# A two-block transformer on one core: in-projection norms applied after the matmuls, and new addresses for the split halves

## What is computed

```python
for layer in range(2):
    h = rms_norm(x, g_mix[layer])        # x * rsqrt(mean(x*x) + 1e-6) * g
    qkv = h @ w_in[layer]                # 1024 -> 3072
    ...                                  # three kinds of attention
    x = x + mix @ w_out[layer]
    h2 = rms_norm(x, g_ffn[layer])
    x = x + conv_gated_mlp(h2, ...)      # up 1024 -> 5632, down 2816 -> 1024
x = rms_norm(x, g_final)
```

## Time and profile before

| | us |
|---|---|
| median of 3 executions | 1744.21 (1742.28 to 1744.73) |
| the profiled execution | 1744.4 |
| its span, first to last instruction | 1742.6 |
| TensorE (PE) busy | 1693.9 |
| VectorE (DVE) busy | 1151.4 |
| ScalarE (ACT) busy | 821.4 |
| GpSimd (POOL) busy | 706.1 |
| mean granted clock of TensorE, share of full | 0.996 |

### The profile page before, as it was taken

How to read it: one execution, slowest core, us unless ns; L and a number is a source line. 1 busy time by engine, 2 the same in 40 slices (tenths; PEclk the granted TensorE clock), 3 DMA queues, 4 the chain that set the end, 5 groups by cost and what they waited for, 6 DMA issues and landing times.

```text
span 1742.6 us, 27224 instructions
## 1 busy us (share of the span) xinstructions
PE 1693.9 (97%) x10714; PEld 1456.7 (84%) x10714; DVE 1151.4 (66%) x2422; ACT 821.4 (47%) x1453; POOL 706.1 (41%) x384
## 2 busy tenths in 40 slices
PE   7999999999999998999999999999999999999997
PEld 6779998777799986544579999999999988888885
DVE  6755785756467585655332999999999644444443
ACT  5555655355476642122343554544444455555553
POOL 2424676133266811421163999700000144444443
PEclk9999999999999999999999999999999999999998
DMA  7333545463165463323353656544444466666664
GB/s 289 117 109 135 191 170 183 148 217 117 61 211 201 170 199 122 107 86 120 97 202 114 225 165 203 179 144 141 144 145 140 162 193 194 194 193 194 194 193 134
DMA packets 77456, 283.20 MB, mean 163 GB/s; under 512 B 8721, under 2 KB 8977, under 8 KB 77073
## 3 DMA queue, kind: packets, MB, share of 16 engines
q1 hardware_dynamic: 76032, 276.50, 48.5%
q10 hardware_dynamic: 1296, 4.97, 0.8%
HBM read 279.33 MB, written 2.10 MB: 161 GB/s over the span
## 4 chain that ended last, share of the span: by engine, by line
PE 79%; DVE 7%; POOL 4%; ACT 4%; issue 3%; DMA 1%; POOLq 0%; DVEq 0%; ACTq 0%
PE bank L542 63%; PE bank L533 8%; PE bank L597 5%; POOL wl L2117 4%; ACT wh L1112 2%; DVE att L1478 2%; PE bank L665 1%; DVE wl L1461 1%; ACT att L1115 1%; PE bank L967 1%; PE bank L889 1%; DVE ssb L1467 1%; DVE mix L1506 1%; DVE xs L1467 1%; PE bank L837 0%
## 5 line engine op out<-in xcount | busy, mean ns | idle before, releaser
L2117 POOL TENSOR_TENSOR wl<-raw,wh 128x1024 fp32r<-128x1024 f32 x213 | 547.6, 2582 | 696.5 <-ACT wh L1112 688.1
L542 PE MATMUL bank<-hh,wh 128*128 128x256 f32 x1856 | 526.5, 284 | 5.1 <-POOL wl L2117 4.2
L1112 ACT ACTIVATE wh<-raw 128x1024 fp32r<-128x1024 f32 x476 | 492.9, 1050 | 58.2 <-PE bank L542 39.4
L542 PE MATMUL bank<-hl,wh 128*128 128x256 f32 x1856 | 519.3, 280 | 0.0
L542 PE MATMUL bank<-hh,wl 128*128 128x256 f32 x1856 | 517.9, 279 | 0.0
L1461 DVE TENSOR_TENSOR wl<-raw,wh 128x1024 fp32r<-128x1024 f32 x263 | 353.8, 1351 | 93.8 <-ACT wh L1112 93.3
L542 PEld LDWEIGHTS bank<-hh,wh 128*128 128x128 f32 x1856 | 349.1, 188 | 6.6 <-POOL wl L2117 5.5
L542 PEld LDWEIGHTS bank<-hl,wh 128*128 128x128 f32 x1856 | 349.2, 188 | 0.0
L542 PEld LDWEIGHTS bank<-hh,wl 128*128 128x128 f32 x1856 | 349.0, 188 | 0.0
L1467 DVE TENSOR_TENSOR acl<-H,ach 128x256 fp32r<-128x256 f32 x128 | 87.6, 685 | 181.5 <-ACT ach L1115 181.5
L542 PE MATMUL bank<-wh,ach 128*128 128x512 f32 x512 | 199.2, 389 | 0.4 <-DVE acl L1467 0.4
(11 more groups left out here) (216 smaller groups left out, 2322.5 us busy)
## 6 DMA issues: line engine op xcount, KB each, us to landing
raw<-in_ut_dram SPq DMA_DIRECT2D x128, 512.0 KB, 3.5
raw<-in_vt_dram SPq DMA_DIRECT2D x128, 512.0 KB, 3.7
raw<-in_wup_dram SPq DMA_DIRECT2D x88, 512.0 KB, 4.1
raw<-in_win_dram SPq DMA_DIRECT2D x48, 512.0 KB, 4.6
raw<-in_wdown_dram SPq DMA_DIRECT2D x44, 512.0 KB, 4.2
raw<-in_wout_dram SPq DMA_DIRECT2D x24, 512.0 KB, 3.6
raw<-in_wga_dram SPq DMA_DIRECT2D x16, 512.0 KB, 3.6
raw<-in_wpq_dram SPq DMA_DIRECT2D x16, 512.0 KB, 4.7
```

The lines of the kernel that those rows point to most:

```text
L542: m = p.e.matmul(out, lhs[i][a], rhs[i][b], start=start and i == 0 and j == 0, stop=stop and i == n - 1 and j == 2)
L1112: a.e.activation(high_of(u), raw_of(u), ACTF.Copy).then_inc(act_hi.up(("hi", u)), 1)
L2117: g.e.tensor_tensor(low_of(u), raw_of(u), high_of(u).bitcast(F32), ALU.subtract).then_inc(pool_lo.up(("lo", u)), 1)
```

## The change

Norm of x before the in projections: the row of weights is no longer multiplied in before the turning. x itself is turned; the weight enters as one column per 128 features (gcol, a new input of 128 x 32 floats) while the halves are made, ACT by a scale and DVE in one scalar_tensor_tensor; that makes one instruction per 128 x 128 block instead of one per 256 or 512 columns. The root per token enters when the in projection's result is evicted. The two rows leave the plan of units. In layer 0 slab 0 is no longer skewed, and 16 further transposes whose result nobody reads are issued behind the turning. Between the layers, tile 0 is turned inside the down projection, before the last unit's matmuls of tile 1 are complete.

Addresses: hh and hl become 9216 bytes each, of which the "f" halves (up projection, pq, ut) use the part from float 16 on and all others the part from 0. sta becomes 3072 bytes, con 6656, sml 3584; a tile gcol of 384 bytes stands ahead of xs; the reserve for dynamic DMA at the partition's start is 1024 bytes (it was 16384 by default).

```diff
-def program(nc, x_d, pos_d, consts_d, smalls_d, win_d, ...
+def program(nc, x_d, pos_d, consts_d, smalls_d, gcol_d, win_d, ...
+        gcol_s = scoped(ctx, "gcol", 96)
...
-        hh, hl = scoped(sc_h, "hh", 2048, F32R), scoped(sc_h, "hl", 2048, F32R)
+        hh, hl = scoped(sc_h, "hh", 2304, F32R), scoped(sc_h, "hl", 2304, F32R)
         sc_h.close()
-        hw, sel_s = scoped(ctx, "hw", 2048), scoped(ctx, "sel_s", 2048)
-        sta = scoped(ctx, "sta", 760)
+        hw, sel_s = scoped(ctx, "hw", 2304), scoped(ctx, "sel_s", 2304)
+        sta = scoped(ctx, "sta", 768)
...
-        con_s = scoped(early, "con", K_W - 128)
-        sml_s = scoped(early, "sml", S_W)
+        con_s = scoped(early, "con", 1664)
+        sml_s = scoped(early, "sml", 896)
...
         for L in range(DEPTH):
-            stage(("row", "n", L), [(rows_d[L], 1024, False)])
...
-                lower.append("pd"[i % 2])
+                lower.append("dp"[i % 2])
...
+        def hT_of(st):
+            o = 16 if st[0] == "f" else 0
+            return [w[:, o:o + 2048].rearrange("p (k t) -> p k t", k=8) for w in (hh, hl)]
+
+        def gcol(st, k):
+            return gcol_s[:, 8 * (st[1] + 2 * (st[0] == "f")) + k:8 * (st[1] + 2 * (st[0] == "f")) + k + 1]
...
+            def x_turned(st, t, k0, b, *after):
+                claim(b)
+                p.wait_ge(*after)
+                n = block_of(st, t, k0)[1]
+                for k in range(k0, k0 + n):
+                    m = p.e.transpose(banks[b][:, (k - k0) * 128:(k - k0) * 128 + 128], x[:, t, k * 128:(k + 1) * 128], ids[:, :])
+                m.then_inc(pe_out.up(("T", st, t, k0)), 1)
...
             p.wait_ge(id_in, "id")
-            turned(("n", 0), mix, 8, (0, 1), lambda t, q: (dve_out, ("nrm", ("n", 0), t, q)))
+            for q in range(2):
+                for t in range(2):
+                    x_turned(("n", 0), t, 4 * q, 2 * q + t, (x0_in, x1_in)[t], "x")
+            turn[0] += 6
+            kept_streaming(16, 5)
...
-                                  lambda n, t: (act_out if t else dve_out, ("ev", "win", L, n, t)), of=slab_banks, skew=(0,),
-                                  between=(lambda: turned(("n", 1), mix, 8, (1,), ...)) if L else None, at=(3, 0))
+                                  lambda n, t: (act_out if t else dve_out, ("ev", "win", L, n, t)), of=slab_banks, skew=(0,) if L else (),
+                                  between=(lambda: [x_turned(("n", 1), 1, 4 * q, rot(), dve_out, ("xd", 0, 1, q)) for q in range(2)]) if L else None, at=(3, 0))
...
+                        if L == 0 and (f, t, n) == (NTILE - 2, 1, 0):
+                            spare = [(acc[1][1] + i) % 8 for i in (1, 2)]
+                            for q in range(2):
+                                x_turned(("n", 1), 0, 4 * q, spare[q], dve_out, ("xd", 0, 0, q))
...
+            def x_high(st, t, ks):
+                for k in ks:
+                    a.wait_ge(pe_out, ("T", st, t, block_of(st, t, k)[0]))
+                    a.wait_ge(g_in, "g")
+                    do(hT_of(st)[0][:, k, tcols(t)], turned_block(st, t, k), ACTF.Identity, ("hTh", st, t, k), scale=gcol(st, k))
...
             load(ids[:, :], consts_d[:, 0:128], id_in, "id")
+            load(gcol_s[:, 0:32], gcol_d, g_in, "g")
             load(pos_i, pos_d, pos_in, "pos")
             for t in range(2):
+                x_high(("n", 0), t, range(4))
+            stream_up_to(first["win", 0] + 1)
+            load(con_s[:, 0:K_W - 128], consts_d[:, 128:K_W], con_in, "con")
+            load(sml(0, S_W), smalls_d, sml_in, "sml")
+            for t in range(2):
+                x_high(("n", 0), t, range(4, 8))
+            stream_up_to(first["win", 0] + 2)
+            for t in range(2):
                 squares(("n", 0), t, x[:, t, :], mix[:, t, :], 0, (x0_in, x1_in)[t], "x")
-            stream_up_to(first["win", 0])
-            load(con_s[:, :], consts_d[:, 128:K_W], con_in, "con")
-            load(sml(0, S_W), smalls_d, sml_in, "sml")
-            turned(("n", 0), (0, ), 2)
-            stream_up_to(first["win", 0] + 1)
-            turned(("n", 0), (1, ), 2)
-            stream(0)
...
                         a.wait_ge(pe_out, ("mm", ("win", L), k // 4, 1))
-                        do(qkv[:, 1, ...], ps(("win", L), k // 4, 1), ACTF.Copy, ("ev", "win", L, k // 4, 1))
+                        a.wait_ge(pool_out, ("rs", ("n", L), 1))
+                        do(qkv[:, 1, ...], ps(("win", L), k // 4, 1), ACTF.Identity, ("ev", "win", L, k // 4, 1), scale=rstd[:, 1:2])
...
+            def x_low(st, t, ks):
+                for k in ks:
+                    v.wait_ge(act_out, ("hTh", st, t, sum(block_of(st, t, k)) - 1))
+                    v.wait_ge(g_in, "g")
+                    v.e.scalar_tensor_tensor(hT_of(st)[1][:, k, tcols(t)], turned_block(st, t, k), gcol(st, k), hT_of(st)[0][:, k, tcols(t)].bitcast(F32),
+                                             ALU.mult, ALU.subtract).then_inc(dve_out.up(("hT", st, t, k)), 1)
...
             for t in range(2):
+                x_low(("n", 0), t, range(4))
+            stream_up_to(first["win", 0])
+            for t in range(2):
+                x_low(("n", 0), t, range(4, 8))
+            stream_up_to(first["win", 0] + 2)
+            for t in range(2):
                 mean(("n", 0), t, False)
-                scale(("n", 0), t, mix, first["row", "n", 0])
-            stream_up_to(first["win", 0])
-            turned(("n", 0), (0, 1), 2)
-            stream(0)
...
-                        copy(qkv[:, 0, ...], ps(("win", L), k // 4, 0), ("ev", "win", L, k // 4, 0), alone=True)
+                        v.wait_ge(pool_out, ("rs", ("n", L), 0))
+                        v.e.tensor_scalar(qkv[:, 0, ...], ps(("win", L), k // 4, 0), rstd[:, 0:1], None, ALU.mult
+                                          ).then_inc(dve_out.up(("ev", "win", L, k // 4, 0)), 1)
...
-            for t in range(2):
-                root(("n", 0), t)
-            g.wait_ge(dve_out, ("nrm", ("n", 0), 1, 1))
-            stream(0)
...
                     if k < 23:
                         stream(first["win", L] + k)
+                    if k == 0:
+                        if L == 0:
+                            root(("n", 0), 0)
+                        root(("n", L), 1)
...
-                            root(("n", 1), t)
-                            g.wait_ge(dve_out, ("nrm", ("n", 1), t, 1))
+                            if t == 0:
+                                root(("n", 1), 0)
...
-    nc = _bacc.Bacc("TRN2", target_bir_lowering=False, num_devices=1)
+    nc = _bacc.Bacc("TRN2", target_bir_lowering=False, num_devices=1, dynamic_dma_scratch_size=1024)
```

More of the change, by code:

```diff
@@ L250, in program @@
             else:
-                L = 0 if i < first["row", "n", 1] else 1
-                if first["row", "n", L] + 7 <= i < first["wdown", L] - 5 and not (L == 0 and i < first["win", 0] + 6):
+                L = 0 if i < first["win", 1] else 1
+                if first["win", L] + 6 <= i < first["wdown", L] - 5 and not (L == 0 and i < first["win", 0] + 6):
                     lower.append("ddp"[i % 3])
@@ L821, in pe @@
                 if L == 0:
-                    turned(("n", 1), mix, 8, (0,), lambda t, q: (dve_out, ("nrm", ("n", 1), t, q)), of=[b for b in range(8) if b not in acc[1]])
+                    turn[0] += 3
             turned_whole(("n", 2), hn2, (0, ))
```

93 lines of the change are left out of this document (51 added, 42 removed).

## The result

The changed kernel takes 1751.57 us (median of 6 executions, 1749.78 to 1757.73), the kernel before 1744.47 on the same chip (1741.94 to 1746.20): a ratio of 1.0056, 95% interval 1.0045 to 1.0067. The change makes it slower by 0.56% (0.41% by the medians; two of the six executions took over 1757 us), where I had forecast 1720 us. The profiled execution took 1749.78 us around its span of 1748.0; before it was 1744.4 around 1742.6.

A forecast was written before the change was run, and what follows sets the result against it. TensorE, busy 1693.9 of 1742.6 us, was taken to bound the kernel. The homes, entry and layer boundary terms sum to 24.2 us off the median of 1744.2, giving 1720 us, with a range of 1707 to 1745.

The forecast's parts named there:

- Homes: Address part: tiles starting at one place modulo 512 save some 7 ns per 512-column matmul; "f" halves sit 64 bytes off.
- (a): Down projections: the 512-column step falls from 233.4 and 228.3 to 226.6 ns, a gain of 2.7 us.
- (b): In and out projections: step from 233.4 to 226.6 ns; two thirds of 5.9 us taken, a gain of 3.9 us.
- Rival D: Everywhere: position has nothing to do with the step; 0.2 us left, 1744 us; chance 0.13.
- (c): "f" halves, 64 bytes off: 256-column step falls to 113.3 ns; gains: up projections 10.1 us, pq 1.8, ut 5.5.
- My discount for DVE: ut's other 69 units: half of their 7.4 us counted, because DVE is busy 40.0 of 40 us from 1260.
- Rival B: "f" halves: 64 bytes is like any other difference, 256-column steps stay at 118 ns; 1737 us; chance 0.20.
- Rival C: "f" halves: 64 bytes brings the full hindrance, 120.2 ns a step, so slower; 1750 us; chance 0.12.
- Entry: Kernel start through slab 0, with raw x turned and a wait for gcol: -0.7 us, between -2 and +1.7.
- Layer boundary: Between layers: no POOL wait for the scaled row, tile 0 turned in the down projection; TensorE's idle goes, 0.9 us gained.

The follow-up runs named there:

- homes_only: The kernel before with the new addresses alone ("f" halves at 64 bytes), old norms, plan and slots: 1738.41 us, ratio 0.9978.
- homes_192: The kernel before with the new addresses alone, but the "f" halves at 192 bytes instead of 64: 1737.38 us, ratio 0.9959.
- entry_repaired: slots_back with DVE's low half ahead of the small steps, ACT's sines one unit later, POOL only units 1 and 3 of the first 12: 1743.30 us.
- slots_back: The changed kernel with the unit slots ahead of ut moved back by two, as before the change: 1747.03 us, ratio 1.0016.
- halves_back: slots_back with each unit's low half made by the same engine as in the kernel before: 1744.81 us, ratio 1.0011.

## Why the prediction was wrong

- **Homes, (a) and (b).** Right in size of the step: 226.5 ns was measured for 226.6. The size: down projections 2.0 us (0.8 and 1.2 in homes_only) for 2.7, since layer 0 still waits 0.37 and 1.39 us for POOL. In and out projections some 1.7 us for 3.9 (0.35, 0.23, 0.11, 0.77 and 0.24 in the table's rows): attention paces more of them than the third I had taken. Rival D, that position does nothing, is out: by addresses alone (homes_only) the in projection's step went from 233.4 to 226.7 ns, 24 steps from 350.12 to 355.56 us. The Trainium skill (TensorE: Matmul & The Clock Gate, Step-by-step: what each phase is for) says that streamed data and weights come through two independent ports and loading weights takes nothing from the running matmul, which would have made D right; the measurement decides against it. How the two reads hinder each other no run shows.
- **Homes, (c), the step that failed.** I took 113.3 ns for the "f" halves at 64 bytes: I carried the floor from one form to the other and called every other difference a hindrance of one size. I also read one step per difference from the trace before, where ut already ran mostly at 116.7 ns, at the same 32 bytes as the up projection's 117.8 (96 steps):
```profile
1059.83 0.28 PE L542 MATMUL bank<-hh,wh 128*128 128x256 f32 x1
...
1071.03 0.28 PE L542 MATMUL bank<-hh,wh 128*128 128x256 f32 x1
```

There are at least five levels (113.3, 116.7, 117.8, 118.7, 120.0), and at 64 bytes two of them. Up projections: 0.4 us for 10.1. pq: 1.7 in homes_only for 1.8. ut: 3.3 won in its first part at 113.3, 1.55 lost in the rest, where the step went from 116.7 to 117.8, for 5.5. My discount for DVE there stays untested at the floor, but in homes_192, with every second unit at 113.3, TensorE had no wait from 1130 to 1370 us. Rival B was right about the up projections alone. Rival C had the right sign, and its 1750 us are within 2 us of the result by luck: 120.0 exists, but not at 64.
- **A gain that had no place to go.** In homes_192, where up projection 1 ran at 113.3, two thirds of it came back as waits for POOL one stage later; in entry_repaired, with other engines for the low halves, nothing did. I had asked what is late next for ut, and not for the up projection.
- **Entry.** First matmul 14.72 us for 14.2. gcol came at 8.9, not 9.8, but an ACT table load of 1.28 us stood behind it, which I had left out. Slab 0 ended at 25.8 for 26.8, better than forecast. The failed step is that I stopped the sum there: the loss of 4.35 us lies in slab 1, where unit 4's low half stood on DVE behind small steps slowed by POOL's two low halves, a queue I had not walked through. The half clock behind the wait was not in the sum.
- **Layer boundary.** Forecast +0.9. The first slab of layer 1 lost 2.66 us, because the halving of the rows stands in ACT's queue ahead of four wh's; the cover I had named (down matmuls and the slab) needs those wh's itself. Down projection 0 won more than the addresses give it, so that the two stages together gained 0.6 us over homes_only (76.63 to 76.04 in slots_back). But that gain is the shifted engines': with the engines as before (halves_back) the two take 78.37 us, a loss of 1.7.
- **Not in the sum at all.** Two units fewer in the plan shift every rule in `i % n`: the slots (7.2 us at ut's start, 4.5 of the median, 0.40% by the ratios) and the halves' engines (3.9 us at the entry and 4.0 at the attention's start, against 2.4 won in down projection 0; 2.2 of the median, 0.05% by the ratios). I put this at nothing without a reason. It takes the ratio from 1.0056 to 1.0011; what is left between that and homes_only's 0.9978 is the new norms' own entry (about 1 us up to slab 3), the boundary, levels of the step that differ by execution (1.7 us in pq), and a rest that the runs don't split.

## What to carry to other kernels

Taking an element out of a list whose consumers are chosen by `i % n` changes all that follow: print slots and engines of both versions and compare them before costing anything. A matmul's step depends on where its operands lie, and has to be measured for each form: the best difference of one form was among the worst of the other. A faster stage is worth only what its own supply and that of the next stage allow, so add up both before counting the gain.

## What was unexpected of the hardware

- Same form, same addresses modulo 512, granted clock 1.00, one execution: 113.3 ns in one stretch and 117.8 in another, each constant over hundreds of steps. At 64 bytes the level changed at waits or single long steps of TensorE, in both directions, and 22 extra matmuls did not change it; at 192 bytes it alternated from unit to unit, with eight short matmuls between and no wait.
- 256-column form: 120.0 ns at differences of 0, 96 and 256 bytes, 113.3 or 117.8 at 64 and 192; 512-column form: 226.6 at 0.
- Two DVE steps of 24 elements took 2.5 us while POOL made a low half, and 0.39 behind it. What looks like a bundle of cheap steps cost as much time as POOL's two low halves.
- The half clock lasted 3.4 us behind waits of 1.84 and 2.77 us, and 6.8 us at the wait of 6.99 us, 3.0 of them inside it. Behind the wait of 1.81 us at 348 us there was none, and behind the same wait of 1.81 us in entry_repaired (at 342.2 us) there was one of 3.4 us.
